# Four blocks of the first layer turned by VectorE's quadrants instead of TensorE, and residual copies in three steps

## The chip, the cores and the metric

The kernel runs on one core of a Trainium2 chip, as one program. The metric is the device time of one execution in microseconds; before the change it is 1991.52 us, the median of three runs.

## The reference

The reference is a two-layer trunk for one sequence of 256 tokens with width 2048, all in float32. Cut to what matters here:

```python
# layer 0: h = rmsnorm(x)
proj = h @ w_in                         # 2048 x 6144
q, k, v, g, xb, gate = split(proj)      # 1024 columns each
q = rotary(q) * dk**-0.5; k = rotary(k) # 8 heads of 128
ret_out = norm(retention(q, k, v)) * silu(g)
lru_out = rg_lru_block(conv(xb), ...) * gelu(gate)
x = x + concat(ret_out, lru_out) @ w_out
x = x + relu(rmsnorm(x) @ w_up)**2 @ w_down      # hidden width 8192
# layer 1: sliding window attention instead of the mixer, then an MLP
# last: a final rmsnorm
```

The retention multiplies q and k per head with the head's 128 features on the contracted side, and the LRU is a scan over tokens. So q, k, gate and xb are wanted with features on the partitions and tokens along the row, while the projection gives tokens on the partitions. Each of them has to be turned.

## The kernel before

**Blocks and slots.** All products with weights are cut into 89 blocks of 512 output columns (`BLOCKS`, line 78). Blocks 0 to 11 are the first layer's input projection in the order xb0, gate0, q0, k0, v0, g0, xb1, gate1, q1, k1, v1, g1 (the digit is the half), blocks 12 to 15 its output projection ("res"), then come 32 blocks of the first MLP, five of q, k and v of the attention, four of its output projection (53 to 56) and 32 of the second MLP. While TensorE multiplies block b, the other engines work on the result of block b - 1; this stretch is slot b. So "the slot behind q1" is slot 9, in which TensorE multiplies k1. It has eight weight steps (k = 0 to 7).

**A weight step.** Weights and activations are split into a high and a low float32r part, and a product is three matmuls (lines 1635 to 1637: high by high, low by high, high by low). A step covers 256 rows of a block's weights, 12 matmuls of 128x512. For each step ScalarE writes `w_hi` (`cut_hi`, line 841) and VectorE `w_lo`, the difference (`cut_lo`, line 1144), into a ring of four places. Both run four steps ahead: in iteration k of their loop they make step k + 4, and `w_hi` of that step waits until TensorE has used the place (step k). TensorE waits on `lo_ready` for each step. The MLPs replace some products by a recursion with sums of weights and tokens (`PAIRS0`, lines 1640 to 1665), whose sums VectorE also adds (L1155 to L1162).

**The order within an iteration** is written out by hand and the same in each engine's `body`: first what belongs to the block behind (`post`, `behind`), then the LRU, retention or attention step, then the `w_hi` or `w_lo`. Each engine takes its instructions strictly in that order.

**Behind a block of the input projection.** In iteration 0 ScalarE's `leave` moves the accumulator to `stage` (L896). For q and k VectorE rotates `stage` into `turn` in iteration 1 (`rotate`, L1272 to L1277; signal `rotated`). TensorE's `post` (line 1758) then turns eight 128x128 tiles with the identity into `bank` (L1753), behind step 4 for q, k and g, behind step 2 for gate (`TURN_AT`), and in the next iteration VectorE copies both halves from the bank to `q_t`, `k_t` or `gate_t` (L1510), signal `turned_out`. The blocks xb, kv and aq (`DIRECT`) go another way: `turn_quadrants` (line 1400) turns 16 pieces of 32x256 by VectorE's transpose (L1425) straight from `stage` to the target tile, as many in each iteration as `QUADRANTS_AT` says, and signals `turned_out` itself. `leave` waits for that signal before it overwrites `stage`.

**The LRU** takes one of eight feature groups in each of slots 2 to 5 and 8 to 11. VectorE's convolution (L1304, L1307) is in iteration 1 or 2 (`CONV_AT`), TensorE's two gate products (L1784, L1785) stand behind step 4, and wait for it. ScalarE's sigmoids (L943, L946) are in iteration 5, the rest in 6 and 7, and VectorE's scan is in iteration 0 of the next slot. GpSimd does a polynomial of the gate (L809 to L811), which starts when `turned_out` tells that gate is in `gate_t`; ScalarE waits for it (`poly_done`) in iteration 5.

**Behind the residual blocks.** VectorE adds the accumulator to `x` (L1475). For blocks 13 to 15 and 54 to 56 (`moved_by_act`) ScalarE then copies the 16 pieces of 32x256 of the new residual to `shifted` (`move_res`, L933), four in each of iterations 1 to 4 (`RES_MOVED_AT`), or in iterations 3 to 8 for the block right before an MLP (`RES_AT`). One iteration after the last copies VectorE turns `shifted` with four transposes of 128x256 (`turn_shifted`, L1442), and in the one behind that both engines split the result (`turned_parts`, L851 on ScalarE and L1239 on VectorE) into the activations of the next stage.

Of the kernel before, what the change touches and what calls it, by code (L numbers as in the profile page):

```python
# [35 lines left out]
NB = 512  # L36
# [10 lines left out]
TAPS = 4  # L47
# [32 lines left out]
NBLK = len(BLOCKS)  # L80
# [10 lines left out]
DIRECT = {"xb", "kv", "aq"}  # L91
# [3 lines left out]
PLAIN = TURNED - SPLIT - DIRECT  # L95
FROM_STAGE = {"gate"}

TURN_AT = {"q": 4, "k": 4, "g": 4, "gate": 2}
# [8 lines left out]
SQUARES_PAIR = {3: 2, 4: 2, 5: 2, 6: 2, 7: 2, 8: 2, 9: 2, 10: 2}  # L107
RES_AT = {3: 5, 4: 1, 5: 1, 6: 2, 7: 5, 8: 2}
RES_MOVED_AT = {1: 4, 2: 4, 3: 4, 4: 4}
MOVED_SUMS_AT = 7  # L110
# [187 lines left out]
def quadrants_at(kind, b):  # L298

    if kind == "up":  # L300
        return QUADRANTS_UP if b in UP0 else {}
    if moved_by_act(b):
        return {}
    at = QUADRANTS_EARLY if b == ATT_OUT0 else QUADRANTS_AT[kind]
    return {k + late(b): n for k, n in at.items()}
# [9 lines left out]

INIT_HALVES = 2 * COLS
X_TURN_AT = {2: 2, 4: 3}
ZEROS_GROUPS = 2
# [5 lines left out]
N_TURNED = total(TURNED, 2)  # L324
N_MOVED = total(TURNED - DIRECT, 2)
N_SPLIT = total(SPLIT, 2)
# [95 lines left out]
def build(nc, t):  # L422
    ctx = ExitStack()
    with ctx:
# [51 lines left out]
        gate_t = take(LG, SEQ)  # L476
# [345 lines left out]
        def _(act):  # L822
# [45 lines left out]
            def leave(slot, kind, j):  # L868

                b = slot.b - 1  # L870
                if b not in UP0 | UP1:
                    act.wait_ge(half_used, slot.halves(late(b)))
                if b > 0 and BLOCKS[b - 1][0] in DIRECT:

                    act.wait_ge(turned_out, slot.count(N_TURNED, -1, INIT_HALVES))
# [249 lines left out]
        def _(dve):  # L1125
# [274 lines left out]
            def turn_quadrants(slot, k, kind, j):  # L1400
# [10 lines left out]
                if k == min(at) and kind == "res":  # L1411
                    dve.wait_ge(evac_dve, slot.count(N_EVAC_DVE, 0))
                if k == min(at) and kind in DIRECT:
                    dve.wait_ge(evac_act, slot.count(N_EVAC_ACT, 0))
                src = x[:, :, j * NB:(j + 1) * NB] if kind == "res" else part_l if kind == "up" else stage
                src = src.rearrange("p t (k f c) -> p t k f c", k=COLS, f=QUADRANTS)
                if kind in DIRECT:
                    tile = {"xb": xb_t[:, :, TAPS - 1:], "kv": kk_t, "aq": qq_t}[kind]
                    dst = tile.rearrange("p k (t a c) -> p t k a c", t=TT, a=QUADRANTS)
                else:  # L1420
                    dst = turn.rearrange("p m (k t a c) -> p t (m k) a c", k=2, t=TT, a=QUADRANTS)
# [5 lines left out]
                if k == max(at):  # L1427
                    ins.then_inc(turned_out if kind in DIRECT else turned, 2)

# [36 lines left out]
            def behind(slot, k):  # L1466
# [12 lines left out]
                if k == 1 + late(b):  # L1479
# [11 lines left out]
                    if kind == "kv":  # L1491
# [5 lines left out]
                        nc.vector.tensor_copy(v_even[CHUNK:P, 1, :], v_att[0:CHUNK, 1, :]).then_inc(values_ready, 1)  # L1497
                if kind in BY_VECTOR:
                    turn_quadrants(slot, k, kind, j)
                if kind == "up" or moved_by_act(b):  # L1500
                    turn_shifted(slot, k, kind)
                if kind in TURNED and k == out_at(kind, b):
                    for m in range(2):
                        if kind in SPLIT:
                            hi, lo, kt, scale = target(b)
                            turned_parts(hi, lo, kt + 2 * m, None if scale is None else scale + 2 * m,
                                         slot.count(N_SPLIT, -1, INIT_HALVES + m + 1), m, kind in BY_VECTOR)
                        elif kind in PLAIN:
                            dve.wait_ge(turned, slot.count(N_MOVED, -1, INIT_HALVES + m + 1))
                            nc.vector.tensor_copy(plain_target(kind, j)(m),  # L1510
                                                  bank[:, m, :].rearrange("p (k s) -> p k s", k=2)
                                                  ).then_inc(turned_out, 1)
# [101 lines left out]
        def _(pe):  # L1614
# [143 lines left out]
            def post(slot):  # L1758

                b = slot.b - 1  # L1760
                kind, j = BLOCKS[b]
                if kind not in TURNED - BY_VECTOR:
                    return
# [3 lines left out]
                elif kind in "qk":  # L1767
                    pe.wait_ge(rotated, {("q", 0): 1, ("k", 0): 2, ("q", 1): 3, ("k", 1): 4}[(kind, j)])
                    src = turn
# [205 lines left out]
```

## Time and profile before

| | |
|---|---|
| median of three runs | 1991.52 us (1991.15 to 1991.54) |
| profiled execution, its own time | 1991.4 us |
| its span in the profile | 1989.6 us |
| TensorE busy | 1977.4 us |
| VectorE busy | 1528.1 us |
| ScalarE busy | 1274.9 us |
| GpSimd busy | 45.1 us |

The span is what the profile covers, from the first instruction to the last; 1.8 us of the execution lie around it. Times in the rows below are microseconds from the start of the span. The timeline merges neighbours of the same kind: `x3` is three instructions and the duration is that of all. In brackets stands the idle time of the engine before the row, and what ended it. Matmuls overlap, so the distance of two starts is the cost of one, not the duration that is listed.

### The profile page before, as it was taken

How to read it: one execution, taken by the hardware profiler on the slowest of the kernel's cores; microseconds unless marked ns; L12 is line 12 of the kernel's file. 1: busy time of each engine (PE TensorE's matmuls, PEld its weight loads, DVE VectorE, ACT ScalarE, POOL GpSimd, SP SyncE). 2: the span in 40 equal slices, each digit the busy share in tenths (PEclk: the TensorE clock that was granted, in tenths of full speed). 3: DMA queues.
4: the chain of work that ended last, by engine and by line, in shares of the span. 5: the costliest groups of instructions: out<-in, count | busy, mean ns of one | idle time of the engine just before them, and what ended most of it. 6: DMA issues, size and time to landing. Idle time of an engine off the chain costs nothing.

```text
span 1989.6 us, 25376 instructions
## 1 busy us (share of the span) xinstructions
PE 1977.4 (99%) x9041; PEld 1626.0 (82%) x9041; DVE 1528.1 (77%) x1968; ACT 1274.9 (64%) x1866; POOL 45.1 (2%) x55
## 2 busy tenths in 40 slices
PE   9999999999999999999999999999999999999998
PEld 7888888788888888888888878878888888888887
DVE  7777777887778877778689887888777778777765
ACT  6665665878558646745855566778647755854764
POOL 1110110000000000000000000000000000000000
PEclk9999999999999999999999999999999999999999
DMA  8556546474655457556555544554566556466663
GB/s 307 190 170 217 170 169 209 132 241 157 237 195 182 169 191 246 179 208 209 191 191 191 170 162 161 185 191 148 191 222 220 190 190 211 148 214 225 195 206 112
DMA packets 191759, 382.51 MB, mean 192 GB/s; under 512 B 6328, under 2 KB 7616, under 8 KB 191552
## 3 DMA queue, kind: packets, MB, share of 16 engines
q1 hardware_dynamic: 190288, 377.51, 55.9%
q0 software_dynamic: 1216, 3.88, 0.6%
q8 instruction: 48, 0.79, 0.2%
q14 instruction: 31, 0.25, 0.0%
q10 hardware_dynamic: 176, 0.07, 0.0%
HBM read 379.34 MB, written 2.10 MB: 192 GB/s over the span
## 4 chain that ended last, share of the span: by engine, by line
PE 95%; DVE 2%; ACT 2%; issue 1%; DMA 0%; ACTq 0%; SPq 0%
PE acc L1635 22%; PE acc L1636 22%; PE acc L1637 22%; PE bank L1635 5%; PE bank L1636 5%; PE bank L1637 5%; PE acc L1664 2%; PE acc L1663 2%; PE acc L1665 2%; PE bank L1665 1%; PE bank L1663 1%; PE bank L1664 1%; ACT w_hi L841 1%; ACT area L933 1%; DVE area L1425 1%; DVE w_lo L1144 1%
## 5 line engine op out<-in xcount | busy, mean ns | idle before, releaser
L1144 DVE TENSOR_TENSOR w_lo<-raw,w_hi 128x1024 fp32r<-128x1024 f32 x768 | 929.8, 1221 | 413.0 <-ACT w_hi L841 408.6
L841 ACT ACTIVATE w_hi<-raw 128x1024 fp32r<-128x1024 f32 x768 | 799.9, 1058 | 577.3 <-PE acc L1637 335.6
L1635 PE MATMUL acc<-w_hi,a_hi 128*128 128x512 f32 x1232 | 483.0, 392 | 0.3
L1636 PE MATMUL acc<-w_lo,a_hi 128*128 128x512 f32 x1232 | 479.7, 389 | 0.0
L1637 PE MATMUL acc<-w_hi,a_lo 128*128 128x512 f32 x1232 | 479.6, 389 | 0.0
L1635 PE MATMUL acc<-w_hi,b_hi 128*128 128x512 f32 x784 | 306.1, 390 | 0.0
L1636 PE MATMUL acc<-w_lo,b_hi 128*128 128x512 f32 x784 | 305.2, 389 | 0.0
L1637 PE MATMUL acc<-w_hi,b_lo 128*128 128x512 f32 x784 | 305.1, 389 | 0.0
L1635 PEld LDWEIGHTS acc<-w_hi,a_hi 128*128 128x128 f32 x1232 | 231.3, 188 | 50.2 <-DVE area L1174 1.1
L1637 PEld LDWEIGHTS acc<-w_hi,a_lo 128*128 128x128 f32 x1232 | 231.2, 188 | 48.3
L1636 PEld LDWEIGHTS acc<-w_lo,a_hi 128*128 128x128 f32 x1232 | 231.3, 188 | 47.6
L1635 PEld LDWEIGHTS acc<-w_hi,b_hi 128*128 128x128 f32 x784 | 147.2, 188 | 32.9 <-issue 2.3
L1637 PEld LDWEIGHTS acc<-w_hi,b_lo 128*128 128x128 f32 x784 | 147.2, 188 | 30.8
L1636 PEld LDWEIGHTS acc<-w_lo,b_hi 128*128 128x128 f32 x784 | 147.2, 188 | 30.0
L1636 PE MATMUL bank<-w_lo,b_hi 128*128 128x512 f32 x288 | 112.6, 391 | 0.0
L1635 PE MATMUL bank<-w_hi,b_hi 128*128 128x512 f32 x288 | 112.5, 391 | 0.0
L1637 PE MATMUL bank<-w_hi,b_lo 128*128 128x512 f32 x288 | 112.3, 390 | 0.0
L916 ACT ACTIVATE area<-stage 32x256 f32<-32x256 f32 x256 | 106.3, 415 | 3.9
L1635 PE MATMUL bank<-w_hi,a_hi 128*128 128x512 f32 x192 | 75.4, 393 | 0.8 <-DVE w_lo L1144 0.6
L1636 PE MATMUL bank<-w_lo,a_hi 128*128 128x512 f32 x192 | 75.0, 391 | 0.0
L1637 PE MATMUL bank<-w_hi,a_lo 128*128 128x512 f32 x192 | 74.9, 390 | 0.0
L1663 PE MATMUL acc<-w_hi,s_hi 128*128 128x512 f32 x160 | 63.4, 396 | 1.7 <-DVE w_lo L1144 1.7
(273 smaller groups left out, 1989.9 us busy)
## 6 DMA issues: line engine op xcount, KB each, us to landing
raw<-in_mlp_w_up SPq DMA_DIRECT2D x128, 1024.0 KB, 5.6
raw<-in_mlp_w_down SPq DMA_DIRECT2D x128, 1024.0 KB, 5.1
raw<-in_hyb_w_in SPq DMA_DIRECT2D x44, 1024.0 KB, 5.2
raw<-in_attn_w_qkv SPq DMA_DIRECT2D x20, 1024.0 KB, 5.2
raw<-in_hyb_w_out SPq DMA_DIRECT2D x16, 1024.0 KB, 5.1
raw<-in_attn_w_out SPq DMA_DIRECT2D x16, 1024.0 KB, 5.1
raw<-in_hyb_w_in SPq DMA_DIRECT2D x5, 512.0 KB, 9.8
out_y<-x SPq DMA_DIRECT2D x4, 512.0 KB, 3.0
```

The source lines that it names most:

```text
L841: nc.scalar.activation(w_hi[:, ring(b, h)], raw[:, q, 2 * e:2 * e + 2, :], ACT.Copy).then_inc(hi_ready, counts(b, h))
L916: ins = nc.scalar.activation(shifted[f * QUAD:(f + 1) * QUAD, a], src[a * QUAD:(a + 1) * QUAD, :, :, f, :], ACT.Square)
L933: ins = nc.scalar.activation(shifted[f * QUAD:(f + 1) * QUAD, a], src[a * QUAD:(a + 1) * QUAD, :, :, f, :], ACT.Copy)
L1144: nc.vector.tensor_tensor(w_lo[:, ring(b, h)], raw[:, q, 2 * e:2 * e + 2, :], w_hi[:, ring(b, h)].bitcast(F32), ALU.subtract).then_inc(lo_ ...
L1425: ins = nc.vector.transpose(dst[f * QUAD:(f + 1) * QUAD, :, :, a, :], src[a * QUAD:(a + 1) * QUAD, :, :, f, :])
L1635: nc.tensor.matmul(a, xh, wh, start=first, stop=False, skip_group_check=joins)
L1636: nc.tensor.matmul(a, xh, wl, start=False, stop=False, skip_group_check=joins)
L1637: ins = nc.tensor.matmul(a, xl, wh, start=False, stop=last, skip_group_check=joins)
L1663: nc.tensor.matmul(a, xh, wh, start=first, stop=False, skip_group_check=True)
L1664: nc.tensor.matmul(a, xh, wl, start=False, stop=False, skip_group_check=True)
L1665: ins = nc.tensor.matmul(a, xl, wh, start=False, stop=False, skip_group_check=True)
```

## The change

Four blocks of the first layer, q0 (2), gate1 (7), q1 (8) and k1 (9), are turned by VectorE's quadrant transposes straight into `q_t`, `gate_t` and `k_t`, as xb is. TensorE's eight transposes for each of them and VectorE's two copies are left out. The 16 transposes stand in iterations 2, 3 and 4 (5, 5 and 6 of them) for q and k, in 1, 2 and 3 (4, 6 and 6) for gate1. The evacuation by ScalarE that follows each of these blocks waits until they are done. gate0, k0 and both g stay with TensorE.

The residual copies of blocks 13, 14, 54 and 55 stand in three iterations (5, 6 and 5) instead of four; the turning and the split behind them follow one iteration earlier. For the block before each MLP the 16 copies are spread a little differently over the same six iterations.

```diff
@@ -94,6 +94,15 @@
+MIX_DIRECT = {MIX_IN.index(what): at for what, at in ((("q", 0), {2: 5, 3: 5, 4: 6}), (("gate", 1), {1: 4, 2: 6, 3: 6}),
+                                                     (("q", 1), {2: 5, 3: 5, 4: 6}), (("k", 1), {2: 5, 3: 5, 4: 6}))}
+
+
+def directly(b):
+
+    return BLOCKS[b][0] in DIRECT or b in MIX_DIRECT
@@ -105,8 +114,8 @@
-RES_AT = {3: 5, 4: 1, 5: 1, 6: 2, 7: 5, 8: 2}
-RES_MOVED_AT = {1: 4, 2: 4, 3: 4, 4: 4}
+RES_AT = {3: 4, 4: 2, 5: 1, 6: 2, 7: 4, 8: 3}
+RES_MOVED_AT = {1: 5, 2: 6, 3: 5}
@@ -301,6 +310,8 @@
+    if b in MIX_DIRECT:
+        return MIX_DIRECT[b]
@@ -870,7 +882,7 @@
-                if b > 0 and BLOCKS[b - 1][0] in DIRECT:
+                if b > 0 and directly(b - 1):
 
                     act.wait_ge(turned_out, slot.count(N_TURNED, -1, INIT_HALVES))
@@ -1410,12 +1422,15 @@
-                if k == min(at) and kind in DIRECT:
+                if k == min(at) and directly(slot.b - 1):
                     dve.wait_ge(evac_act, slot.count(N_EVAC_ACT, 0))
-                src = x[:, :, j * NB:(j + 1) * NB] if kind == "res" else part_l if kind == "up" else stage
+                if k == min(at) and kind in "qk":
+                    dve.wait_ge(rotated, ROTATED[(kind, j)])
+                src = (x[:, :, j * NB:(j + 1) * NB] if kind == "res" else part_l if kind == "up" else
+                       turn if kind in "qk" else stage)
                 src = src.rearrange("p t (k f c) -> p t k f c", k=COLS, f=QUADRANTS)
-                if kind in DIRECT:
-                    tile = {"xb": xb_t[:, :, TAPS - 1:], "kv": kk_t, "aq": qq_t}[kind]
+                if directly(slot.b - 1):
+                    tile = {"xb": xb_t[:, :, TAPS - 1:], "kv": kk_t, "aq": qq_t, "gate": gate_t, "q": q_t, "k": k_t}[kind]
@@ -1425,7 +1440,7 @@
-                    ins.then_inc(turned_out if kind in DIRECT else turned, 2)
+                    ins.then_inc(turned_out if directly(slot.b - 1) else turned, 2)
@@ -1495,7 +1510,7 @@
-                if kind in BY_VECTOR:
+                if kind in BY_VECTOR or directly(b):
                     turn_quadrants(slot, k, kind, j)
@@ -1505,7 +1520,7 @@
-                        elif kind in PLAIN:
+                        elif kind in PLAIN and not directly(b):
@@ -1759,13 +1774,13 @@
-                if kind not in TURNED - BY_VECTOR:
+                if kind not in TURNED - BY_VECTOR or directly(b):
                     return
```

## Rows read from the trace of the kernel before

**Rows 1.** The page's part 1: busy time, share, instructions of each engine.

```profile
PE 1977.4 (99%) x9041; PEld 1626.0 (82%) x9041; DVE 1528.1 (77%) x1968; ACT 1274.9 (64%) x1866; POOL 45.1 (2%) x55
```

**Rows 2.** Windows behind gate1, q1, k1: busy PE, PEld, DVE, ACT, POOL, clock, DMA.

```profile
197.24:220.85 23.61, 23.61 (x109) 19.61 (x108) 12.86 (x15) 13.74 (x17) 3.33 (x4) 1.00 0.55 180
220.85:244.37 23.52, 23.52 (x109) 19.61 (x108) 20.09 (x29) 16.05 (x21) 4.67 (x4) 1.00 0.52 178
244.37:267.90 23.53, 23.53 (x109) 19.61 (x108) 20.09 (x29) 16.05 (x21) 4.67 (x4) 1.00 0.52 181
```

**Rows 3.** VectorE's timeline behind q1: start, duration, engine, line, operation, count, idle.

```profile
234.19 1.22 DVE L1144 TENSOR_TENSOR w_lo<-raw,w_hi 128x1024 fp32r<-128x1024 f32 x1
235.32 0.42 DVE L1332 TENSOR_TENSOR b_lo<-area,b_hi 128x256 fp32r<-128x256 f32 x1
235.66 3.49 DVE L1144 TENSOR_TENSOR w_lo<-raw,w_hi 128x1024 fp32r<-128x1024 f32 x3
239.06 1.28 DVE L1510 COPY area<-bank 128x512 f32<-128x512 f32 x2
```

**Rows 4.** TensorE's timeline behind q1, around its eight transposes.

```profile
234.46 1.03 PE L1753 MATMUL bank<-ident,turn 128*128 128x128 f32 x8
235.33 0.60 PE L1784 MATMUL bank<-area 128*128 128x256 f32 x2
...
236.01 0.58 PE L1635 MATMUL acc<-w_hi,a_hi 128*128 128x512 f32 x1
236.43 0.40 PE L1636 MATMUL acc<-w_lo,a_hi 128*128 128x512 f32 x1
```

**Rows 5.** Groups by line and form, VectorE, 0 to 420: busy, mean ns | idle.

```profile
L1425 DVE STREAM_TRANSPOSE area<-stage 32x256 f32<-32x256 f32 x32 | 13.9, 436 | 0.5
...
L1510 DVE COPY area<-bank 128x512 f32<-128x512 f32 x12 | 7.7, 681 | 0.0
```

**Rows 6.** VectorE's timeline behind xb0, a `w_lo` and two batches of transposes.

```profile
39.88 1.23 DVE L1144 TENSOR_TENSOR w_lo<-raw,w_hi 128x1024 fp32r<-128x1024 f32 x1
41.13 2.68 DVE L1425 STREAM_TRANSPOSE area<-stage 32x256 f32<-32x256 f32 x6
43.82 1.23 DVE L1144 TENSOR_TENSOR w_lo<-raw,w_hi 128x1024 fp32r<-128x1024 f32 x1
```

**Rows 7.** Timelines of ScalarE, VectorE and TensorE ahead of the second MLP.

```profile
1258.45 1.70 ACT L933 ACTIVATE area<-x 32x256 f32<-32x256 f32 x4 [1.74 <-DVE x L1475]
...
1276.08 1.28 DVE L1475 TENSOR_TENSOR x<-x,acc 128x512 f32<-128x512 f32 x2
...
1277.39 1.70 ACT L933 ACTIVATE area<-x 32x256 f32<-32x256 f32 x4 [0.59 <-DVE x L1475]
...
1288.60 1.22 DVE L1144 TENSOR_TENSOR w_lo<-raw,w_hi 128x1024 fp32r<-128x1024 f32 x1 [1.58 <-ACT w_hi L841]
...
1303.50 1.22 DVE L1144 TENSOR_TENSOR w_lo<-raw,w_hi 128x1024 fp32r<-128x1024 f32 x1
...
1304.78 0.50 PE L1663 MATMUL acc<-w_hi,s_hi 128*128 128x512 f32 x1 [0.78 <-DVE w_lo L1144]
1305.12 0.39 PE L1664 MATMUL acc<-w_lo,s_hi 128*128 128x512 f32 x1
```

**Rows 8.** Timelines of VectorE, GpSimd and ScalarE behind gate1.

```profile
201.32 1.23 DVE L1144 TENSOR_TENSOR w_lo<-raw,w_hi 128x1024 fp32r<-128x1024 f32 x1 [1.55 <-ACT w_hi L841]
...
209.51 0.61 POOL L809 TENSOR_TENSOR junk<-area 128x256 f32<-128x256 f32 x1 [58.92 <-DVE area L1510]
...
210.69 1.58 POOL L811 TENSOR_TENSOR junk<-junk,area 128x256 f32<-128x256 f32 x1
...
213.72 0.41 ACT L946 ACTIVATE junk<-junk 128x256 f32<-128x256 f32 x1
215.61 1.06 ACT L841 ACTIVATE w_hi<-raw 128x1024 fp32r<-128x1024 f32 x1 [1.48 <-PE acc L1637]
```

**Rows 9.** The page's part 6: DMA issues, KB each, us to landing.

```profile
raw<-in_hyb_w_in SPq DMA_DIRECT2D x44, 1024.0 KB, 5.2
```

More of the change, by code:

```diff
@@ L316 @@
 INIT_HALVES = 2 * COLS
+ROTATED = {("q", 0): 1, ("k", 0): 2, ("q", 1): 3, ("k", 1): 4}
 X_TURN_AT = {2: 2, 4: 3}
@@ L324 @@
 N_TURNED = total(TURNED, 2)
-N_MOVED = total(TURNED - DIRECT, 2)
+N_MOVED = [2 * sum(BLOCKS[n][0] in TURNED and not directly(n) for n in range(b)) for b in range(NBLK + 1)]
 N_SPLIT = total(SPLIT, 2)
@@ L1767, in post @@
                 elif kind in "qk":
-                    pe.wait_ge(rotated, {("q", 0): 1, ("k", 0): 2, ("q", 1): 3, ("k", 1): 4}[(kind, j)])
+                    pe.wait_ge(rotated, ROTATED[(kind, j)])
                     src = turn
```

## The prediction

> **What bounds the kernel now.** I read the page's busy shares first: TensorE is busy 99% of 1989.6 us and VectorE 77% [rows 1]. So TensorE is the bound, and work taken from it is worth its full duration, provided that the engine which takes it over has room at that place. The average doesn't answer that, so next come the windows by slot. In the slot behind block q1 VectorE is busy 20.09 of 23.52 us, behind gate1 only 12.86 of 23.61 [rows 2]; the slot behind k1 repeats q1's numbers, and so does, in the timeline, the one behind q0. Third is VectorE's timeline in q1's slot [rows 3]: the order inside one slot, where each `w_lo` of a weight step has to be out before TensorE starts that step. That is the view on which most of this prediction rests.
>
> **Names.** A slot is eight weight steps of 12 products. VectorE's and ScalarE's iteration k makes `w_lo` and `w_hi` of step k+4, so VectorE can be up to about three steps late before TensorE sees it. A slot with a turning and a pair of LRU gates takes 23.52 us [rows 2]; the turning and the gates take 0.87 each (below), so a step is (23.52 - 1.74) / 8 = 2.72 us.
>
> **What leaves TensorE.** Eight transposes stand between two products: they start at 234.46, the next group at 235.33, so they cost 0.87 us, and the gates behind them start at 235.33 and the product at 236.01, which is followed after 0.42 instead of 0.23 us: 0.87 again [rows 4]. Four blocks lose their turning: 4 x 0.87 = 3.5 us, the whole possible gain, 0.18%.
>
> **What comes to VectorE.** A quadrant transpose of 32x256 takes 436 ns, a copy of a bank 681 ns [rows 5]. Six in a row advance the engine from 41.13 to 43.82, 0.449 each, and the step from `w_lo` to the first of them is 1.25 instead of 1.14 [rows 6]. A block is 16 x 0.449 + 3 x 0.11 = 7.5 us, against two copies that go (1.28 us at 239.06 [rows 3]): 6.2 us more for each of four blocks. The source in `turn` or `stage` and the target in `area` have the shape of those measured rows, so I take the same price; no row shows another. In q1's slot VectorE then wants 20.1 + 6.2 = 26.3 us in a slot that would last 22.7. It can't fit; what is left is how much its lead hides.
>
> The Trainium skill says the same from the other side ("VectorE: DVE Perf Modes", Rules for kernel authors): for a 128x128 transpose use TensorE if PSUM will do. Its table of the three transpose paths prices a 128x128 bf16 turning at 311 ns on VectorE and 390 ns on TensorE; by these a block would be an estimated 8 x 0.311 - 1.28 = 1.2 us more on VectorE, which the slots could hold, and that is the result of the first rival below. The float rows here say 16 x 0.449 for eight such tiles, some 0.9 us each, and they decide.
>
> **q0 and q1, step by step** (q1's times; q0's slot repeats them 143.17 us earlier). A product starts 1.28 us after the start of its `w_lo` when it had waited for it (1303.50 to 1304.78 [rows 7]), and then loses 0.11 more to refilling (0.34 instead of 0.23 to the next). Rotation and convolution fill iteration 1 until 234.19, when `w_lo` of step 5 starts [rows 3]; it is ready at 235.47. Today TensorE needs it at 236.01, a margin of 0.5 us. Without the turning TensorE is there at 235.33, so 0.1 of the gain is a stall at once.
> - Step 6: 234.19 + 1.14, five transposes with their start (2.36), `b_lo` (0.34, 235.32 to 235.66 [rows 3]): `w_lo` starts at 238.02, ready at 239.30; TensorE is free at 238.3. Stall 1.0.
> - Step 7: + 1.14 + 2.36: 241.52, ready 242.80; TensorE free at 242.1. Stall 0.7.
> - Step 0 of the next slot: + 1.14 + 2.80: 245.46, ready 246.74; TensorE free at 245.6. Stall 1.1.
>
> With the refills the next slot begins at 246.8 instead of 244.37. A q slot is thus 2.4 us longer, not 0.87 shorter. After q0 comes k0 with its old copies; VectorE begins that slot 0.7 us later in relation to TensorE than today, inside the margin, and nothing more is lost or given back. q0: +2.4.
>
> **gate1, then q1 and k1.** VectorE has room behind gate1, and no product waits: 4, 6 and 6 transposes in iterations 1 to 3 with the convolution among them push the last `w_lo` of these only to 214.1, ready long before step 7 of a slot that began at 197.24 (TensorE there at 217). That is -0.87. But GpSimd waits for the same signal. Today the copies end at 209.4, GpSimd starts its three operations at 209.51 and takes 2.8 us, and ScalarE's sigmoid of them runs at 213.72, with time to spare before `w_hi` at 215.61, which waits for TensorE [rows 8]. With the transposes the signal comes later: the slot's first `w_lo` starts at 201.32 [rows 8], and behind it stand 1.25, 4 x 0.449, `w_lo` 1.14, six transposes 2.8, the convolution 1.9, `w_lo` 1.14 and six transposes 2.8, so it comes at 214.1; GpSimd is done at 217.0, and ScalarE, in order, holds its `w_hi` behind the sigmoid until 217.5. Its next two iterations (3.15 and 2.6 us with their table loads) and the evacuation leave no pause, so it enters q1's slot 2 us late, and VectorE's rotation and convolution there end at 236.0 instead of 234.19, with TensorE at its gates already at 233.5: a stall of 2.6 us. From then on VectorE is the bound through two slots: the stalls of q1's list, then k1 from a later phase. VectorE's own time decides: k1's slot begins at 248.7 and v1's at 275.2, today 244.37 and 267.90. Together gate1, q1 and k1: +7.3 us. Behind k1 come v1 and its retention, whose margins of 0.3 us and more I count as kept.
>
> **The waits added.** ScalarE's evacuation of k0, q1, k1 and v1's bank now waits until VectorE has turned the block before. Queued behind it are the `w_hi` of that slot. The last transposes of q1 end about when TensorE ends the slot (1.1 us before step 0 starts), so it costs 0 to 0.3 us; I take 0. The weight transfers start when a `w_lo` is out; a unit is wanted seven iterations (19 us) later and lands in 5.2 [rows 9], so 4 us of lateness doesn't reach them. 0.
>
> **The residual copies.** ScalarE makes 16 copies of 0.42 us in three iterations instead of four, and VectorE's turning (1.35) and split (1.6) come one iteration earlier. The number of operations is the same; only lateness moves. At the second MLP's entry there is no slack: TensorE already waits 0.78 us at 1304.78 for a `w_lo` whose chain of solid VectorE work goes back to 1288.60, and that goes back to copies that start at 1277.39 when the residual add is out [rows 7]. One block earlier the copies start at 1258.45 [rows 7]. In three iterations of 5, 6 and 5, with 1.08 for each `w_hi`, ScalarE is through at 1268.5 and has only the next `w_hi`, until 1269.6; VectorE's `w_lo` and turning end at 1271.0; ScalarE pauses until then, splits (1.6), and its two `w_hi` with the sums (1.4) between them end at 1276.2. Then `w_lo` 1.14 and the add: it starts at 1277.35 instead of 1276.08 [rows 7], and the last chain starts and ends that much later, with 0.1 to 0.2 more from the same exchange inside it. Bounds: -0.8 (the marked wait of 1304.78 gone) and +2.0. I take +1.4, since the worked chain has no pause left to shorten. At the first MLP the same sum ends 0.1 later, since its ScalarE has pauses. Four instead of five copies ahead of one `w_hi` save up to 0.4 twice, but the next wait, for the split of the last block, follows and takes it: 0.
>
> **Sum.** +2.4 + 7.3 + 1.4 + 0.1 = +11.2 us. The profiled execution took 1991.4 with a span of 1989.6, the median is 1991.52: I predict 2002.7.
>
> **Rivals.**
> - *The lead hides it* (not slower). VectorE's additions stay under the three steps (8 us) by which `w_lo` may be late, so no product waits. For it: four of eight iterations have pauses, and behind xb0 the same 16 transposes cost TensorE nothing. Against: in q slots the margin of step 5 is 0.5 us before the first transpose. It decides at a transpose batch of under some 1.5 us for an iteration (0.25 each), where I count 2.4. Time: -3.5, with the residual part -0.8 to +1.4: 1987.2 to 1989.4. Chance 0.13, of it 0.04 below 1987.5.
> - *GpSimd's late signal costs nothing* (ScalarE catches up before q1): gate1 keeps -0.9, q1 and k1 cost 5.6 from q1's normal phase: 4.7 + 2.4 + 1.5 = +8.6, 2000.1. Chance 0.17.
> - *Partly hidden*: transposes out of `turn` overlap better or the phase recovers between slots: half of the stalls, 1995 to 1999. Chance 0.09.
> - *It spills over*: k0's slot or the retention behind k1, with margins of 0.3 to 0.7 us, stall too, each up to 2.5 us: 2005.5 to 2008. Chance 0.08.
> - Forecast 2002.7 (2000.5 to 2005.5): 0.53.
>
> A measurement can tell about 0.2%, 4 us, from no change: faster is below 1987.5, same up to 1995.5. Faster 0.04, same 0.10, slower 0.86. Range 1995.5 to 2006.
>
> **What would show it.** Right: waits of product L1635 for `w_lo` L1144 in the slots behind q0, q1 and k1, at steps 5, 6, 7 and 0; GpSimd's first operation near 214; v1's slot some 10 us later than today (2.4 of it from q0). Wrong: no such waits there, transposes out of `turn` well under 0.44, or ScalarE's `w_hi` behind the sigmoid at its old distance.

## The result and the profile after

The changed kernel takes 2007.12 us (median of 6 runs, 2006.03 to 2008.13), the kernel before, on the same chip, 1991.48 (6 runs, 1991.15 to 1993.33). The ratio is 1.0075, with a 95% interval of 1.0064 to 1.0086: slower by 0.64 to 0.86%, where 2002.7 with a range up to 2006.0 was predicted. The profiled execution took 2006.8 us with a span of 2005.0, so +15.4 us of span is what the trace has to account for.

The page's part 1 of the changed kernel, and the first line of its part 4, the chain that ended last:

```profile
PE 1980.8 (99%) x9009; PEld 1623.8 (81%) x9009; DVE 1552.3 (77%) x2024; ACT 1273.8 (64%) x1866; POOL 44.5 (2%) x55
PE 84%; DVE 9%; ACT 4%; issue 2%; DMA 0%; POOL 0%; ACTq 0%; SPq 0%
```

Beside [rows 1]: TensorE has 32 instructions fewer (the four turnings), VectorE 24 us more (64 transposes came, eight copies went). The shares have hardly moved. The chain has: VectorE now holds 9% of it; before it was 2% (PE 95%). The waits of TensorE in the changed kernel (engine, line, who released it: us in total, times, longest):

```profile
PE acc L1650 <- DVE w_lo L1156: 6.5, 8, 1.2
PE bank L1799 <- DVE area L1319: 3.9, 2, 3.3
PE bank L1650 <- DVE w_lo L1156: 1.9, 1, 1.9
```

L1650 is the product of a weight step (L1635 before), L1156 its `w_lo`, L1799 the gate product, L1319 the convolution that it reads. The windows of the slots behind q1 and k1, to be held against the second and third line of [rows 2]:

```profile
223.10:253.06 29.96, 25.11 (x101) 19.39 (x100) 26.21 (x43) 19.48 (x25) 4.15 (x4) 0.94 0.42 136
253.06:280.38 27.32, 24.03 (x100) 18.39 (x101) 26.38 (x43) 16.04 (x20) 3.97 (x4) 1.00 0.46 153
```

A slot of 23.52 us has become one of 29.96, the next one of 27.32, and VectorE is busy 26.2 to 26.4 us in each: 6.1 to 6.3 more than before, the 6.2 of the prediction.

**Where the 15.4 us lie.** I matched each product of the one trace with the same product of the other and read how much later it starts. The shift changes only at these places:

| stretch | shift at its end | gained there | predicted |
|---|---|---|---|
| start of the program | 0.43 | 0.43 | 0 |
| q0's slot and k0's | 3.17 | 2.74 | 2.4 |
| gate1's turning | 2.19 | -0.98 | -0.87 |
| q1's slot | 8.69 | 6.50 | 5.2 |
| k1's slot | 12.48 | 3.79 | 3.0 |
| retention behind it | 12.76 | 0.28 | 0 |
| first MLP's entry | 12.58 | -0.18 | 0.1 |
| second MLP's entry | 14.49 | 1.91 | 1.4 |
| last transfers of the output | 15.40 | 0.91 | 0 |

(The prediction gives gate1, q1 and k1 together as +7.3, with k1's slot beginning at 248.7 and v1's at 275.2; the split follows from these.) The first line lies in a stretch that the change doesn't touch: in the profiled executions of the experiments it was between -0.1 and 2.0. The last line is another matter. The last transfer of `out_y` lands 4.19 us after its issue, before the change 3.33, and this isn't scatter: it is 4.2 in all four profiled programs that turn the four blocks whole (2024 VectorE instructions), and 3.3 in the other ten. In these four a packet of the queue that loads instructions (q14) starts 2.8 us before the end, while that transfer runs; in the kernel before there is none. So these 0.9 us come with the change as well, and no forecast had them. That the packet delays the transfer isn't shown: the two versions with gates in pieces, below, have such a packet 4.1 us before the end and land in 3.3. The change is 15.0 us against 11.2.

**q0.** TensorE's timeline in q0's slot, changed kernel (start, duration, ..., idle before and its releaser):

```profile
96.43 0.50 PE L1650 MATMUL acc<-w_hi,a_hi 128*128 128x512 f32 x1 [0.70 <-DVE w_lo L1156]
99.93 0.50 PE L1650 MATMUL acc<-w_hi,a_hi 128*128 128x512 f32 x1 [0.45 <-DVE w_lo L1156]
104.01 0.47 PE L1650 MATMUL acc<-w_hi,a_hi 128*128 128x512 f32 x1 [1.06 <-DVE w_lo L1156]
```

These are steps 6, 7 and 0, the three that were named, at 0.70, 0.45 and 1.06 us where 1.0, 0.7 and 1.1 were worked out.

**q1.** VectorE's timeline there:

```profile
233.17 1.10 DVE L1284 TENSOR_TENSOR turn<-stage,rope 128x512 f32<-128x512 f32 x1
234.19 0.88 DVE L1285 TENSOR_TENSOR area<-stage,rope 128x512 f32<-128x512 f32 x1
235.00 1.22 DVE L1286 TENSOR_TENSOR turn<-stage,rope 128x512 f32<-128x512 f32 x1
...
238.51 1.53 DVE L1319 SCALAR_TENSOR_TENSOR area<-area,vecs 128x256 f32<-128x256 f32 x3
239.95 1.22 DVE L1156 TENSOR_TENSOR w_lo<-raw,w_hi 128x1024 fp32r<-128x1024 f32 x1
241.09 2.22 DVE L1440 STREAM_TRANSPOSE area<-turn 32x256 f32<-32x256 f32 x5
243.33 0.42 DVE L1344 TENSOR_TENSOR b_lo<-area,b_hi 128x256 fp32r<-128x256 f32 x1
243.67 1.76 DVE L1156 TENSOR_TENSOR w_lo<-raw,w_hi 128x1024 fp32r<-128x1024 f32 x1
245.46 2.23 DVE L1440 STREAM_TRANSPOSE area<-turn 32x256 f32<-32x256 f32 x5
247.70 1.23 DVE L1156 TENSOR_TENSOR w_lo<-raw,w_hi 128x1024 fp32r<-128x1024 f32 x1
248.96 2.70 DVE L1440 STREAM_TRANSPOSE area<-turn 32x256 f32<-32x256 f32 x6
```

No line has an idle time: VectorE works without a pause. The transposes out of `turn` cost what [rows 6] said: six in 2.70 us. One term is new: the `w_lo` of 243.67 took 1.76 us instead of 1.22. GpSimd's product of L825 ran beside it, from 243.43 for 0.92.

TensorE in the same stretch, then the windows of one microsecond each around it (busy PE, PEld, DVE, ACT, POOL, then the granted clock, DMA share and GB/s):

```profile
240.09 1.22 PE L1799 MATMUL bank<-area 128*128 128x256 f32 x2 [3.31 <-DVE area L1319]
241.11 1.06 PE L1800 MATMUL bank<-area 128*128 128x256 f32 x2
241.61 0.99 PE L1650 MATMUL acc<-w_hi,a_hi 128*128 128x512 f32 x1
...
243.23 0.39 PE L1650 MATMUL acc<-w_hi,a_hi 128*128 128x512 f32 x1
```

```profile
239.00:240.00 1.00, 0.00 (x0) 0.00 (x0) 0.93 (x3) 0.24 (x1) 0.00 (x0) 0.89 0.00 0
240.00:241.00 1.00, 0.91 (x2) 0.82 (x3) 1.00 (x2) 0.00 (x0) 0.00 (x0) 0.50 0.02 8
242.00:243.00 1.00, 1.00 (x4) 0.81 (x3) 0.97 (x3) 0.79 (x3) 0.00 (x0) 0.50 0.53 74
243.00:244.00 1.00, 1.00 (x6) 0.79 (x5) 0.99 (x3) 0.35 (x2) 0.57 (x1) 0.91 0.90 311
```

The predicted stall ahead of the gates is there, 3.31 us instead of 2.6, and something that wasn't predicted comes with it: while TensorE stood still the granted clock fell to 0.50 (1.2 GHz) and it stayed there until 243. From the gates to the fourth product it took 3.14 us, before 1.56 (from 235.33 [rows 4] to 236.89 in the same timeline): 1.58 us of low clock. It is hidden here, because VectorE is the bound: TensorE comes to step 6 only some 0.2 us before its `w_lo` is out, so the low clock stands where the next stall would have stood, and k1's slot begins when VectorE is through.

**The signal chain behind gate1**, GpSimd's and ScalarE's timelines:

```profile
217.22 1.64 POOL L821 TENSOR_TENSOR junk<-area 128x256 f32<-128x256 f32 x1 [63.54 <-DVE area L1440]
218.96 1.25 POOL L822 TENSOR_SCALAR junk<-junk 128x256 f32<-128x256 f32 x1
220.29 0.74 POOL L823 TENSOR_TENSOR junk<-junk,area 128x256 f32<-128x256 f32 x1
...
221.06 0.42 ACT L958 ACTIVATE junk<-junk 128x256 f32<-128x256 f32 x1 [5.07 <-POOL junk L823]
221.39 1.05 ACT L853 ACTIVATE w_hi<-raw 128x1024 fp32r<-128x1024 f32 x1
```

GpSimd begins at 217.22; predicted was 214.1, plus the shift of 3.17 that is there already: 217.27. It then takes 3.81 us instead of the 2.8 of [rows 8], because it now stands beside two `w_lo` (217.17, 2.78 us for the two instead of 2.36). So the sigmoid, and `w_hi` behind it in ScalarE's order, start about 0.8 us later than worked out.

### The profile page after: what moved, and what is told of

Its sections match the earlier page's. It is cut to its first block, busy times and chain, and to the rows that moved or that the text cites. A ratio compares the mean times of both kernels' runs of the same rounds, so it can differ in the third digit from the quotient of the medians.

```text
span 2005.0 us, 25353 instructions
## 1 busy us (share of the span) xinstructions
PE 1980.8 (99%) x9009; PEld 1623.8 (81%) x9009; DVE 1552.3 (77%) x2024; ACT 1273.8 (64%) x1866; POOL 44.5 (2%) x55
## 4 chain that ended last, share of the span: by engine, by line
PE 84%; DVE 9%; ACT 4%; issue 2%; DMA 0%; POOL 0%; ACTq 0%; SPq 0%
PE acc L1650 19%; PE acc L1651 19%; PE acc L1652 19%; PE bank L1650 5%; PE bank L1651 5%; PE bank L1652 5%; DVE w_lo L1156 3%; PE acc L1679 2%; PE acc L1678 2%; PE acc L1680 2%; DVE area L1440 2%; ACT w_hi L853 2%; ACT area L945 1%; PE bank L1680 1%; PE bank L1679 1%
## 5 line engine op out<-in xcount | busy, mean ns | idle before, releaser
L1156 DVE TENSOR_TENSOR w_lo<-raw,w_hi 128x1024 fp32r<-128x1024 f32 x768 | 931.7, 1224 | 405.7 <-ACT w_hi L853 401.3
L1650 PE MATMUL acc<-w_hi,a_hi 128*128 128x512 f32 x1232 | 484.0, 393 | 6.6 <-DVE w_lo L1156 6.5
L1650 PE MATMUL acc<-w_hi,b_hi 128*128 128x512 f32 x784 | 306.2, 391 | 0.0
L1650 PEld LDWEIGHTS acc<-w_hi,a_hi 128*128 128x128 f32 x1232 | 231.6, 188 | 61.2 <-DVE w_lo L1156 7.3
L1650 PEld LDWEIGHTS acc<-w_hi,b_hi 128*128 128x128 f32 x784 | 147.1, 188 | 33.0 <-issue 2.5
L1650 PE MATMUL bank<-w_hi,b_hi 128*128 128x512 f32 x288 | 112.5, 391 | 0.0
L1650 PE MATMUL bank<-w_hi,a_hi 128*128 128x512 f32 x192 | 75.6, 394 | 2.7 <-DVE w_lo L1156 1.9
```

The source lines that it names most:

```text
L1156: nc.vector.tensor_tensor(w_lo[:, ring(b, h)], raw[:, q, 2 * e:2 * e + 2, :], w_hi[:, ring(b, h)].bitcast(F32), ALU.subtract).then_inc(lo_ ...
L1650: nc.tensor.matmul(a, xh, wh, start=first, stop=False, skip_group_check=joins)
```

## The experiments

Where a fence of a diff has before.py's values it is laid on the kernel before, else on the changed kernel. Times are medians beside the kernel before of the same job; +x us are shifts of the same product.

**The residual copies by themselves.**

```diff
-RES_AT = {3: 5, 4: 1, 5: 1, 6: 2, 7: 5, 8: 2}
-RES_MOVED_AT = {1: 4, 2: 4, 3: 4, 4: 4}
+RES_AT = {3: 4, 4: 2, 5: 1, 6: 2, 7: 4, 8: 3}
+RES_MOVED_AT = {1: 5, 2: 6, 3: 5}
```

> The kernel before with the two residual tables alone; every block is turned as before. Theory A (the trace of the changed kernel, by the shift of the same product between the two traces): the second MLP's entry costs 0.9 us at its waits for w_lo and 0.9 more where step L6 waits for the split of the last block, the first MLP's entry gives 0.2 back: 1991.5 + 1.6 = 1993.1. Rival: these shifts came from lateness that the four turned blocks left behind, and the tables alone are worth 0: 1991.5, with the product waits of the second entry as in the kernel before (0.20, 0.60, 0.78).

Measured: 1993.04 us against 1991.84, ratio 1.0006 (0.9997 to 1.0016). In the trace +0.3 at the first MLP and +1.4 at the second, 1.7 in all. The theory's +1.6 holds as a sum, but not its split: the first entry gives its 0.2 back and then loses 0.5 at the wait for the last block's split, and at the second entry that wait costs 0.4 instead of 0.9. The time alone couldn't have told the sum from nothing.

Then `RES_AT` alone:

```diff
-RES_AT = {3: 5, 4: 1, 5: 1, 6: 2, 7: 5, 8: 2}
+RES_AT = {3: 4, 4: 2, 5: 1, 6: 2, 7: 4, 8: 3}
```

> The kernel before with RES_AT alone changed. Prediction: the 0.2 to 0.4 us that the waits at steps L4 and R2 of each MLP's entry lose are taken again by the wait for the last block's split at L6: 0. If the split isn't last there: -0.4 to -0.8.

Measured: 1991.57 against 1993.04, ratio 0.9997 (0.9987 to 1.0006). The trace gains 0.4 us at each MLP's entry; the next wait takes 0.2 of it back at the first and all of it at the second, and in the end nothing is left. By difference the cost of the residual part is thus `RES_MOVED_AT`'s: three iterations instead of four. No run has that table alone.

**q0 by itself**, all else as before:

```diff
-MIX_DIRECT = {... ("q", 0), ("gate", 1), ("q", 1), ("k", 1) ...}
+MIX_DIRECT = {MIX_IN.index(what): at for what, at in ((("q", 0), {2: 5, 3: 5, 4: 6}), )}
```

> The kernel before with q0 alone turned by VectorE. Theory A (overload of VectorE in one slot): waits of 0.7, 0.45 and 1.06 us for w_lo at steps 6, 7 and 0 as in the changed kernel, and +2.5 to +2.8: 1994.2. If the loss needed the other blocks: less than +1.

Measured: 1995.65 against 1991.84, ratio 1.0015 (1.0006 to 1.0025); +2.7 us in the trace, 0.37 of it in k0's slot. Then the same 16 transposes in six iterations, at most three in one:

```diff
+MIX_DIRECT = {MIX_IN.index(what): at for what, at in ((("q", 0), {2: 2, 3: 2, 4: 3, 5: 3, 6: 3, 7: 3}), )}
```

> The kernel before with q0 alone turned by VectorE, its 16 transposes spread over iterations 2 to 7 (2, 2, 3, 3, 3, 3) instead of 5, 5, 6 in 2 to 4. Theory A (what counts is VectorE's total of 26.3 us in a slot of 22.7; pauses behind the batch were filled anyway): the waits move to later steps, and the loss is still +2 to +2.7, 1994.0. Rival C (the batches are the fault, not the total): with 0.9 to 1.35 us an iteration the lead absorbs them, -0.8 to +0.5, 1991.3.

Measured: 1995.62 against 1992.92, ratio 1.0017 (1.0007 to 1.0027); +2.8 us in the trace. No product of q0's slot waits for a `w_lo` now. TensorE waits in k0's slot instead, for the rotation and the convolution (L1288, L1318):

```profile
PE bank L1767 <- DVE turn L1288: 1.9, 1, 1.9
PE bank L1798 <- DVE area L1318: 0.8, 1, 0.8
```

VectorE has no idle time from 83.33 until that convolution is done, so it isn't ScalarE's later evacuation of k0 that holds it up. The batches of five and six aren't to blame: the work is too much for the slot, and spreading it only moves the wait. That also ends the rival *The lead hides it*, which drew its line at the size of a batch.

**gate1.** Alone, all else as before:

```diff
+MIX_DIRECT = {MIX_IN.index(what): at for what, at in ((("gate", 1), {1: 4, 2: 6, 3: 6}), )}
```

> The kernel before with gate1 alone turned by VectorE. Theory A (the signal to GpSimd comes 4 us later, ScalarE holds its w_hi behind the sigmoid and enters q1's slot late): the 0.87 us of the turning are won and more than lost again in q1's slot, where VectorE's convolution ends about 2 us later and TensorE's gate products wait for it; q1 has its copies, so no product behind it overruns by transposes: about +1.5 to +2.5, 1993.0 to 1994.0, with a wait of L1784 for the convolution of 2 to 3 us. Rival B (ScalarE catches up, the loss belongs to q1's own transposes): -0.9, 1990.6, and no such wait.

Measured: 1994.62 against 1991.84, ratio 1.0014 (1.0004 to 1.0024). The trace gains 0.9 us at the turning and loses 2.98 in q1's slot, one slot later. TensorE waits there for the rotation (1.4 us, ahead of q1's own turning) and for the convolution (0.8), 2.2 in all, where 2 to 3 were expected at the convolution alone. Then the changed kernel with gate1 left to TensorE:

```diff
-(("gate", 1), {1: 4, 2: 6, 3: 6}),
```

> The changed kernel with gate1 left to TensorE. Theory A: q1 starts from its normal phase; q0 +2.7, q1 +2.5, k1 +3.3 to +3.8 (its slot in the changed kernel is 27.32 long against 23.53), residual tables +1.6: 1991.5 + 10.1 to 10.6, about 2001.9, 5 us faster than the changed kernel. Rival B (gate1 is the innocent part, worth -0.9): 2008.0, slower than the changed kernel.

Measured: 2002.28 against 1991.84, ratio 1.0054 (1.0037 to 1.0070), span 2000.7. q1's slot is +2.3 us, k1's +3.8, and v1's slot begins 2.95 us earlier than in the changed kernel. So gate1 saves its 0.9 and costs 3 us net. (The medians lie 4.8 us apart, the two traces 4.3: the second MLP's entry holds 0.5 of that and the last transfer of the output 0.9.) The rival *GpSimd's late signal costs nothing* falls.

Is it the signal, or VectorE's 16 transposes? Here GpSimd's three operations behind gate1 read another tile that is ready early (so what goes into that gate's GELU is altered) and wait for nothing late; all transposes stay:

```diff
-                pool.wait_ge(turned_out, INIT_HALVES + N_TURNED[1 + 6 * (n // LG) + 1])
+                pool.wait_ge(turned_out, INIT_HALVES + N_TURNED[1 + 6 * (n // LG) + (n != LG)])
-                g = gate_t[:, n % LG, :]
+                g = xb_t[:, 0, TAPS - 1:] if n == LG else gate_t[:, n % LG, :]
```

> The changed kernel, but GpSimd's polynomial of feature group 4 (the first behind gate1) reads xb1's tile, which is complete a slot earlier, so its signal no longer depends on gate1's turning; the features of that group are wrong, the work is the same. Theory A (the late signal costs 3 to 4 us by way of ScalarE's order): the wait of the gate products for the convolution in q1's slot falls from 3.3 us to under 0.5, and the time by 3.5 to 4 us, to about 2003.3; ScalarE's pause of 5.07 us before its sigmoid is gone. Rival (VectorE's load alone makes that wait): no change, 2007.1.

Measured: 2002.03 against 1992.92, ratio 1.0049 (1.0032 to 1.0066). The wait for the convolution, 3.3 us at its longest in the changed kernel, is 0.5:

```profile
PE bank L1799 <- DVE area L1319: 0.5, 1, 0.5
```

v1's slot begins 4.4 us earlier than in the changed kernel. The transposes of gate1 are free; the signal that leaves them is not.

The next version keeps the computation whole. It doesn't make gate1's signal earlier, but gives GpSimd a second pair of buffers, so that it needn't wait until the LRU step before is done with the first, and no longer works beside VectorE's rotation:

```diff
-        gel, gel2 = junk[:, 0:SEQ], junk[:, SEQ:2 * SEQ]
+        gels = [(junk[:, 0:SEQ], junk[:, SEQ:2 * SEQ])]
+        gel_more = take(2, SEQ)
...
+        gels.append((gel_more[:, 0, :], gel_more[:, 1, :]))
...
-                if n > 0:
-                    pool.wait_ge(lru_done, n)
+                if n > 1:
+                    pool.wait_ge(lru_done, n - 1)
+                gel, gel2 = gels[n % 2]
```

> The changed kernel with a second pair of buffers for GpSimd's polynomial, so that it runs one LRU step ahead and no longer beside the rotation. Theory D (formed after the narrow GpSimd run, where the rotation's four products took 0.70, 0.68, 0.70, 0.68 us against 1.10, 0.88, 1.22, 0.68): each slot of q0, q1 and k1 gets 1.2 us shorter for TensorE, k1's 1.6, k0's 0.3: 4 us less than the changed kernel, 2003. Rival (the width of the operations mattered, not their place): no change.

Measured: 2002.77 against 1993.04, ratio 1.0054 (1.0039 to 1.0070). Its shifts: q0 +1.9 instead of 2.7, q1's slot +5.3 instead of 6.5, k1's +2.2 instead of 3.8. The gates of q1 still wait 2.1 us, behind a signal that is as late as before, and here the granted clock stays at 1.00. v1's slot begins 4.1 us earlier than in the changed kernel (0.5 of it from the start of the program), by shorter slots of q0, q1 and k1 as theory D had it; the time is still 9.7 us above the kernel before.

**Two engines side by side.** GpSimd's operations from the second gate on reach over 16 columns instead of 256:

```diff
+                w = 16 if n >= LG else SEQ
-                link(nc.gpsimd.tensor_tensor(gel[:, :], g, g, ALU.mult))
+                link(nc.gpsimd.tensor_tensor(gel[:, 0:w], g[:, 0:w], g[:, 0:w], ALU.mult))
```

> The changed kernel with GpSimd's operations of the second half on 16 columns instead of 256, so those features are partly wrong; everything else is as it was. Theory A: the signal is ready some 3.4 us earlier, nearly all of the late-signal cost goes, and so does the lengthening of VectorE's two-operand instructions beside GpSimd (b_lo 0.93 instead of 0.42 us, w_lo 1.76 instead of 1.22): about 1 us below the run with the early signal, 2002.3. Rival (the two engines don't disturb each other, the longer rows have another cause): same as the early signal, and those rows stay long.

Measured: 2001.63 against 1992.92, ratio 1.0046 (1.0029 to 1.0063). The time is as expected, but it splits otherwise: the gates still wait 1.1 us, since the transposes end late however short GpSimd is, and k1's slot is +2.16 us instead of +3.79. VectorE's rotation in k1's slot shows why:

```profile
257.70 0.70 DVE L1285 TENSOR_TENSOR turn<-stage,rope 128x512 f32<-128x512 f32 x1
258.33 0.68 DVE L1286 TENSOR_TENSOR area<-stage,rope 128x512 f32<-128x512 f32 x1
258.93 0.70 DVE L1287 TENSOR_TENSOR turn<-stage,rope 128x512 f32<-128x512 f32 x1
```

With GpSimd all but away these are 0.70, 0.68 and 0.70 us; beside it, above at 233.17, they are 1.10, 0.88 and 1.22. That is 1.1 us for the rotation and another 0.5 for the `b_lo` of k1's slot, which took 0.93 us in the changed kernel (at 270.68, beside GpSimd's L825 of 270.60) and 0.43 here: 1.6, the whole difference of that slot. The kernel before has the long rotation too (1.10, 0.88 and 1.22 from 227.40 on), so its 1.1 us are no part of what the change costs; the two versions show what they would save.

**Half the transposes.** Every second transpose of q1 and k1 left out, so half of q and k isn't turned:

```diff
+                    if kind in "qk" and j == 1 and n % 2:
+                        continue
```

> The changed kernel with only 8 of the 16 transposes of q1 and of k1 (each block's other half of q_t and k_t keeps the first half's values, so scores of the second half are wrong). Theory A (VectorE's total in the slot decides): 20.1 + 3.75 - 1.3 = 22.6 us fit into a slot of 22.7, the waits for w_lo at steps 6, 7 and 0 go in both slots, and only the wait for the convolution from the late signal stays: 7 to 8 us less than the changed kernel, about 1999.5. If the waits went down in proportion only: 4 us less, 2003.

Measured: 1998.69 against 1992.92, ratio 1.0032 (1.0021 to 1.0043), span 1997.2. Both slots are free of waits for `w_lo`, k1's slot even gains 0.5; what stays is gate1's signal:

```profile
PE bank L1801 <- DVE area L1319: 3.3, 1, 3.3
```

```profile
240.00:242.00 2.00, 1.87 (x6) 1.32 (x7) 1.98 (x4) 0.71 (x2) 0.00 (x0) 0.83 0.01 4
242.00:244.00 2.00, 2.00 (x7) 1.52 (x6) 1.98 (x3) 0.44 (x2) 0.95 (x1) 0.50 0.80 200
```

q1's slot goes from a shift of 2.24 to 6.76, which is +4.5. The clock falls behind the same wait, and here TensorE is the bound again once the gates are through: the wait alone would be some 2.5 us net of the turning, and the low clock adds about what it cost above, 1.6. The price goes with the number of transposes, as the prediction had it: a half fits, the whole doesn't.

**A version for gain.** On the kernel before, only the two gates by VectorE, in pieces: the first group's part first (16 of 32x64), then the rest (16 of 32x192), with GpSimd released behind the first 16:

```diff
+MIX_DIRECT = {MIX_IN.index(("gate", j)): {1: 16, 2: 5, 3: 5, 4: 6} for j in range(2)}
...
+                if n % LG == 0:
+                    pool.wait_ge(gate_first, n // LG + 1)
...
+                    a, f = divmod(n % 16, QUADRANTS)
+                    ks = slice(0, COLS) if kind != "gate" else slice(0, 1) if n < 16 else slice(1, COLS)
```

> The kernel before with gate0 and gate1 turned by VectorE, and nothing else; of each, 16 small pieces (32x64) of the first feature group come first, in iteration 1, and signal GpSimd by themselves, then 16 pieces of 32x192 in iterations 2 to 4. Theory A (gate's slots have room on VectorE, only the signal was late): both turnings are won, 2 x 0.87, and nothing waits: -1.7, 1989.8. If the small pieces cost much more than their share of 0.11 us each, or the convolution comes too late for the gate products: 0 to +2.

Measured: 2004.96 against 1993.04, ratio 1.0062 (1.0048 to 1.0076). A miss. First the price of a small piece. VectorE's groups by form in this kernel (busy, mean ns | idle):

```profile
L1444 DVE STREAM_TRANSPOSE area<-stage 32x256 f32<-32x256 f32 x32 | 13.9, 436 | 0.5
L1444 DVE STREAM_TRANSPOSE area<-stage 32x192 f32<-32x192 f32 x32 | 11.8, 369 | 0.5
...
L1444 DVE STREAM_TRANSPOSE area<-stage 32x64 f32<-32x64 f32 x32 | 7.5, 236 | 0.4
```

A quarter of the elements costs more than half the time, so a gate in two parts is 19.3/2 = 9.7 us of VectorE instead of 7.0. In the profiled execution the shift up to the second MLP is 5.0 us, nearly all of it in gate0's slot. But this execution took 2009.14 us, the slowest of the five and 4.2 above their median. In it a transfer of weights came late (ScalarE's `w_hi` at 29.33 waits 1.93 us for it), VectorE went through gate0's slot 1.7 us later than in the next version, TensorE waited 2.77 us for the convolution, and its granted clock then stood at 0.50 for 6 us:

```profile
71.00:77.00 6.00, 6.00 (x14) 4.69 (x15) 5.82 (x12) 1.14 (x3) 1.50 (x1) 0.50 0.21 51
```

So the 5.0 us are that execution's. What the median lost, 11.9 us, lies in the second MLP's loop, which the edit doesn't touch, and is told in the last section. With the second pair of buffers from above added (same diff):

> The run with both gates by their first group, plus the second pair of buffers. No product waits in those slots before this edit, so a shorter rotation brings TensorE nothing: the same as the gates alone, within 0.3 us.

Measured: 2004.61 against 1993.04, ratio 1.0062 (1.0049 to 1.0076). The medians of the two versions are 0.35 us apart: about as expected, the buffers bring nothing here. In this trace the shift up to the second MLP is 0.2 to 0.4 us instead of 5.0, which can't be the edit's doing, since in gate0's slot GpSimd still uses its first pair. It shows what the pieces cost without the late start: TensorE waits 1.3 us in gate0's slot, the clock stays at 1.00, and both turnings that were won are lost again. The loop costs 12.9 us. No version beat the kernel before.

## Why the prediction was off

The sign, the mechanism and nearly all of its places were right; the size was 4.4 us short (+15.6 by the medians, +11.2 forecast), and the time lies 1.1 us above the range.

- **What leaves TensorE**: right. At gate1, where nothing else is late at that point, 0.98 us went, and 0.9 with gate1 alone, against 0.87.
- **What comes to VectorE**: right. 0.449 each, 6.2 us more in a slot. The row prices held for a source and a target that no row had shown.
- **q0**: right to 0.3 us. Three waits, at the three steps named; 0.37 us more in k0's slot alone, which had been counted as kept.
- **gate1's signal**: right in its mechanism, its time to 0.05 us, and its effect a slot later (early signal: 4.4 us back). Mis-sized was "GpSimd is done at 217.0": I took its 2.8 us over from [rows 8], where it stood beside other work, and it took 3.81.
- **q1 and k1**: +10.3 us where 8.2 was worked out, the largest failing term. The step that failed is the sum of VectorE's own time by durations from the kernel before: each was measured at another neighbour. 0.8 us from the later signal, 0.5 from a `w_lo` of 1.76, 0.5 from a `b_lo` of 0.93, both beside GpSimd's L825. The 0.3 left is a pause of VectorE in k1's slot, which the sum took as full:

```profile
255.69 1.23 DVE L1156 TENSOR_TENSOR w_lo<-raw,w_hi 128x1024 fp32r<-128x1024 f32 x1 [0.30 <-ACT w_hi L853]
```

ScalarE's `w_hi` stands there behind an activation (L968) that waits for a VectorE result of 253.97, and VectorE waits for it in turn. The narrow GpSimd confirms the `b_lo`: 0.43 again in the same slot.
- **Retention**: +0.28, counted as kept; its margin of 0.3 us was just too short. With the 0.37 of k0's slot this is the small piece of the rival *It spills over* that came true.
- **The residual part**: +1.7 where 1.5 was forecast, by an unlike split. The chain gives +0.9 at the second entry; then the wait for the last block's split, set down as 0, takes 0.8 of shift:

```profile
1336.78 0.50 PE L1650 MATMUL bank<-w_hi,a_hi 128*128 128x512 f32 x1 [0.59 <-DVE a_lo L1251]
```

- **The added waits of ScalarE, the weight transfers**: 0, as said. No wait of TensorE names a DMA of the weights in these slots.
- **The low clock**: not in the prediction at all. It cost nothing here only because VectorE was the bound.
- **The last transfer of the output**: not in the prediction either, +0.9, with an instruction packet beside it. It comes with the change, and its cause is argued only.

Only the 0.43 us at the start are within what the kernel before varies by (medians of 1991.5 to 1993.0 in the jobs above); without them the time would still lie above the range. A slot in which an engine goes from 85% to full has no slack left that absorbs small lateness, and each error of the sum then counts in full and in one direction. The range should have been wider above than below.

## What to carry to other kernels

Before work moves to an engine that is 77% busy on average, add it up slot by slot: what decides is the total against the length of the slot, and neither the lead nor a finer spread changes that. Then follow each signal that leaves the moved work through the queues of the engines that wait for it, because the transposes of gate1 were free and their late signal cost 4 us a slot later. Durations from a trace hold for their neighbours: a two-operand instruction that will come to stand beside GpSimd is priced by a row that stood beside it. And before a loss is read from a trace, see whether the profiled execution is near the median: with the gates in pieces it wasn't, and 5 us of its trace belonged to it alone.

## What the runs showed of the hardware

**VectorE and GpSimd lengthen each other.** A rotation product takes 0.68 to 0.70 us alone, 0.88 to 1.22 beside GpSimd; `w_lo` 1.22 and 1.76; `b_lo` 0.43 and 0.93; GpSimd's first product 0.61 [rows 8] and 1.64. The transposes, with one input, show no such spread: in the version with pieces five of 32x192 take 1.89 us beside two operations of GpSimd (at 66.94) and 1.90 while it is idle (at 71.98). The Trainium skill ("GPSIMD Engine Reference", Key points) says that GpSimd shares its SBUF interfaces with VectorE and contends with instructions of two SBUF inputs; the trace agrees, and the sizes are this case's.

**A wait can lower TensorE's clock, and its length alone doesn't tell when.** Behind the wait of 3.31 us the granted clock was 0.50 for about 3 us, and cost 1.58; behind the wait of 2.1 us with two buffers it stayed at 1.00. But at the second MLP's entry the same product waits 1.9 us in seven of the profiled executions: in the changed kernel and with the residual tables alone the clock stayed at 1.00, in the other five it fell to 0.50 for some 3 us (without cost: behind the waits of this entry the shift is 1.0 us larger in all seven). And in the version with gates in pieces a wait of 2.77 us was followed by 6 us at 0.50, and one of 3.06 us in the second MLP by none, while with two buffers the same product's wait of 3.13 us brought 3 us at 0.50. What decides stays open.

**Instructions have to be loaded, too.** In both versions that turn the two gates in pieces, products in the second MLP's loop wait 3.1 us at 1507 and 2.8 at 1678 (times of the kernel before; one turn of the loop later), with a train of smaller waits behind each: the shift goes from 4.96 to 17.7 us in the first version, 12.7 us. TensorE waits for a `w_lo`, that for VectorE, and VectorE for nothing that an engine did: the product named as the releaser had long been done. The chain of waits of the version with pieces, from 1503:

```profile
1505.48 4.88 issue
1510.37 0.06 DVEq L403
1510.43 2.43 issue
```

The page's part 3 has a queue for instructions. Its lines in the kernel before and in the version with pieces (packets, MB, share):

```profile
q14 instruction: 31, 0.25, 0.0%
```

```profile
q14 instruction: 42, 0.34, 0.1%
```

In the kernel before none of its packets falls into 1495 to 1870; in this version four fall into the 15 us around the gap (1503.8, 1508.5, 1511.0 and 1513.5). The last three stand 2.5 us apart, as do the ends of the two stretches of "issue" (1510.37 and 1512.86). So the time goes together with instructions being loaded again within the loop; that the loading causes the gap is argued from this, and no run tests it. Why a program with 60 more VectorE instructions (2028) does so, and the changed kernel with 2024 doesn't (32 packets, of which only two, at 1511 and 1860, fall into this stretch), no run tells; that stays open.
